# Seven block products in the second feed-forward's up product, reordered token-tile ends, and one product for the index key and the index heads' weights

## The reference, cut to what matters

```python
def conv_ffn(h, w_up, conv_w, conv_b, w_down):
    up = h @ w_up                                   # 512 x 1024 by 1024 x 5632
    up = causal convolution of 3 taps over the tokens(up, conv_w) + conv_b
    val, gate = jnp.split(up, 2, axis=-1)           # 2816 columns each
    return (jax.nn.silu(gate) * val) @ w_down

# in the attention, for its index scores:
qi, ki, wi = index queries (8 heads of 64), index key (64), index heads' weights (8)
score = sum over heads of wi * relu(qi . ki)
```

## Time and profile before

| | |
|---|---|
| time, median of 3 runs | 3673.02 us (3670.11 to 3674.25) |
| the profiled execution | 3677.81 us, of which 3676.0 are the span from the first to the last instruction |
| TensorE busy (PE) | 3330.7 us, 91% of the span |
| VectorE busy (DVE) | 1347.4 us, 37% |
| ScalarE busy (ACT) | 609.4 us, 17% |
| mean granted TensorE clock | 0.966 of full |
| up product matmuls (L2786), both layers | 1408 instructions, 614.2 us |

### The profile page before, as it was taken

One profiled execution on the slowest core, in us unless ns is written; L12 is line 12 of the kernel. 1 busy time (PEld: TensorE's weight loads), 2 busy tenths in 40 slices (PEclk: granted clock), 3 DMA queues, 4 the chain that ended last, 5 costly groups with the idle time before them and its releaser, 6 DMA issues. The chain is left out here.

```text
span 3676.0 us, 48556 instructions
## 1 busy us (share of the span) xinstructions
PE 3330.7 (91%) x21177; PEld 1660.3 (45%) x21177; DVE 1347.4 (37%) x2379; ACT 609.4 (17%) x1204; POOL 8.1 (0%) x40
## 2 busy tenths in 40 slices
PE   6978999898997988888999899999999967999998
PEld 3557787444444333333333344454444434444443
DVE  2245656443022000000000226643666673222256
ACT  2134232110011000000000212242121012211100
POOL 0000000000000000000000000000000000000000
PEclk9989999899997999999999999999999988999999
DMA  6134535211227999999999521103433544212233
GB/s 242 46 122 147 180 124 184 85 57 57 69 98 296 430 430 430 430 431 427 428 428 430 214 73 46 69 7 81 146 116 116 191 142 175 92 51 86 69 131 126
DMA packets 202969, 689.76 MB, mean 188 GB/s; under 512 B 31240, under 2 KB 96252, under 8 KB 176517
## 3 DMA queue, kind: packets, MB, share of 16 engines
q1 hardware_dynamic: 201768, 686.28, 48.0%
q10 hardware_dynamic: 989, 0.36, 0.0%
HBM read 661.94 MB, written 22.31 MB: 186 GB/s over the span
## 5 line engine op out<-in xcount | busy, mean ns | idle before, releaser
L2786 PE MATMUL banks<-h_T,weight_ring 128*128 128x512 f32 x1408 | 614.2, 597 | 5.9 <-PEq L91 5.9
L2786 PEld LDWEIGHTS banks<-h_T,weight_ring 128*128 128x128 f32 x1408 | 268.0, 192 | 338.7 <-issue 338.7
L2061 PE MATMUL banks<-weight_ring,xe_T 128*64 128x512 f32 x1312 | 296.8, 599 | 41.8 <-DMA weight_ring<-in_exp_w 39.5
L2942 DVE SCALAR_TENSOR_TENSOR conv<-banks,cols,conv 128x510 f32<-128x510 f32 (+1 forms) x176 | 131.8, 749 | 334.4 <-ACT conv L2869 329.7
L2061 PEld LDWEIGHTS banks<-weight_ring,xe_T 128*64 128x64 f32 x1312 | 90.5, 137 | 235.4 <-issue 160.3
L2077 PE MATMUL banks<-weight_ring,hid_T 128*64 128x512 f32 x656 | 146.8, 596 | 10.9 <-DMA weight_ring<-in_exp_w 10.9
L2869 ACT ACTIVATE conv<-banks,cols 128x512 f32<-128x512 f32 x88 | 63.7, 773 | 504.4 <-PE banks L2786 504.4
L2382 PE MATMUL banks<-h_T,weight_ring 128*128 128x512 f32 x320 | 142.0, 597 | 0.0
L2061 PE MATMUL banks<-h_T,xe_T 128*64 128x512 f32 x464 | 105.4, 596 | 17.2 <-DMA h_T<-in_exp_w 17.2
L1722 PE MATMUL banks<-h_T,weight_ring 128*128 128x512 f32 x256 | 112.9, 600 | 3.9 <-PEq L91 3.9
L3569 PE MATMUL banks<-weight_ring,h_T 128*128 128x512 f32 x256 | 112.6, 602 | 2.6 <-PEq L91 2.6
(11 more groups left out here) (639 smaller groups left out, 4544.1 us busy)
## 6 DMA issues: line engine op xcount, KB each, us to landing
weight_ring<-in_exp_w SPq DMA_DIRECT2D x123, 2048.0 KB, 15.7
h_T<-in_exp_w SPq DMA_DIRECT2D x41, 2048.0 KB, 15.7
weight_ring<-in_ada_w SPq DMA_DIRECT2D x24, 2048.0 KB, 8.6
weight_ring<-in_ffn_w_up SPq DMA_DIRECT2D x44, 1024.0 KB, 6.7
...
```

The lines of the kernel that those rows point to most:

```text
L2061: mm = pe.matmul(k.ps[64 * half:64 * half + 64, 2 * c + b % 2, :], R.rows[:, e // 2 % 2, kt, (e % 2) * CAP:(e % 2 + 1) * CAP], w[:, r, 512 ...
L2786: mm = pe.matmul(k.ps[:, b + c, :], w[:, c, kt, m * P:m * P + P], hT[:, kt, :], start=kt == 0, stop=kt == 7)
L2942: ins = dve.scalar_tensor_tensor(out=y, in0=k.ps[:, b + c, 0:L - d], scalar=tap(i, c, s), in1=y, op0=ALU.mult, op1=ALU.add)
```

## The change

It has three parts.

**Ends of token tiles.** Shifts move ahead of the root and the norm of the next tile, turns move ahead or into the middle of a product (`middle`), and where the next stage is a feed-forward, its tile 0 is multiplied there, for 256 tokens at a time (`first_unit`). ScalarE loads the square root's table with a dummy instruction first.

```diff
     banks = lambda t: (2 * t, 2 * t + 1)
...
-                        if tail and t >= 2:
-                            T.pe_turn(pe, t - 2, banks(t - 2))
+                        if tail and from_ring and t >= lag:
+                            turn(t - lag)
+                        if tail and not from_ring and t == 2:
+                            turn(0)
...
+            if tail and not from_ring:
+                for t in range(LT):
+                    then(t, (lambda: turn(t + 1)) if t + 1 < LT else None)
+            elif tail and norm:
...
+                    then(t - 2)
+                    turn(t)
...
+            elif tail:
+                then(1, lambda: turn(3))
+                then(3)
...
+            if norm or tail:
+                act.activation(ss[:, 1, 0:1], k.misc[:, 6:7], ACT.Sqrt)
...
                 if tail:
+                    if t >= lag:
+                        T.act_shift(act, t - lag, banks(t - lag))
                     T.act_root(act, t)
-                    if t >= 2:
-                        T.act_shift(act, t - 2, banks(t - 2))
```

```diff
-            pe.matmul(k.ps[:, 2 * t + 1, 0:IDX_HEADS], h, ww[:, kt, 64:72], start=kt == 0, stop=kt == 7)
+            if kt == 3 and middle:
+                middle()
...
+def first_unit(k, n, banks):
+
+    def products(pe, t, middle):
+        two = slice((t - 1) * P, (t + 1) * P)
+        k.ring.wait(pe, n)
+        w = k.ring.chunk(n).rearrange("p (c k n) -> p c k n", c=2, k=8)
+        for c in range(2):
+            for kt in range(8):
+                pe.matmul(k.ps[:, banks[c], two], w[:, c, kt, 0:P], k.hT[:, kt, two], start=kt == 0, stop=kt == 7)
+            if c == 0 and middle:
+                middle()
 
     return products
...
-                    pe.wait_ge(evacuated, s)
+                    k.ring.wait(pe, 1)
+                    w = k.ring.chunk(1)[:, 0:576].rearrange("p (k n) -> p k n", k=8)
                     for kt in range(8):
-                        mm = pe.matmul(out, kiw[:, kt, :], hT[:, kt, :], start=kt == 0, stop=kt == 7)
+                        mm = pe.matmul(out[0:64 + IDX_HEADS, :], w[:, kt, :], hT[:, kt, :], start=kt == 0, stop=kt == 7)
...
+                    if job[0] == "ki":
+                        pe.wait_ge(wi_done, 1)
+                        for t in range(LT):
+                            mm = pe.transpose(k.ps[:, 7, IDX_HEADS * t:IDX_HEADS * t + IDX_HEADS], wi_rows[:, t * P:t * P + P],
+                                              k.sq("eye")[64:64 + IDX_HEADS, 64:64 + IDX_HEADS])
+                        mm.then_inc(wi_turned, 1)
...
+        to_residual(k, lambda kt: oT[:, kt, :], None, [4, 4], 2, False, tail=(k.scales[:, 0, 8:16], k.mod2[:, 0, 24:32], k.hT),
+                    follow=first_unit(k, 2, (0, 1)))
```

```diff
+    bank = lambda i, c: 4 * c if i == 0 and not side else 2 * (i % depth) + c
...
+    plain = FF_T if side else 2
+    half = L // 2
+    low_tokens, high_tokens = slice(0, half), slice(half, L)
+    unit_bank = {1: 5, 6: 6, 7: 7, 5: 1, 2: 0, 4: 4, 3: 2}
+    JOINS = 7
...
-                for i in range(FF_T):
+                for i in range(plain):
...
+                    if i == 0:
+                        pe.sem_inc(products, 1)
+                    else:
...
+                    if side and i == 2:
...
+                    if side and i == 3:
...
+                def block_sum(u, n, left, right):
+                    for kt in range(4):
+                        mm = pe.matmul(k.ps[:, unit_bank[n], low_tokens], left[:, kt, :], right[:, kt, :], start=kt == 0, stop=kt == 3)
+                    mm.then_inc(parts, 1)
...
+                for u in range(len(units)):
+                    a11, a12, a21, a22 = unit_blocks(u)
+                    b11, b12, b21, b22 = token_blocks()
+                    if units[u][1] == 0:
+                        k.ring.wait(pe, units[u][0])
+                    if u:
+                        pe.wait_ge(taken, u)
+                    block_sum(u, 1, a11, b11)
+                    pe.wait_ge(readied, 2 * u + 2)
+                    if u:
+                        pe.wait_ge(joined, JOINS * (u - 1) + 1)
+                    block_sum(u, 6, wsum[:, 1], hsum[:, 1])
+                    if u:
+                        pe.wait_ge(joined, JOINS * (u - 1) + 2)
+                    block_sum(u, 7, wsum[:, 2], hsum[:, 2])
+                    if u:
+                        pe.wait_ge(joined, JOINS * (u - 1) + 4)
+                    block_sum(u, 5, wsum[:, 0], hsum[:, 0])
+                    if u:
+                        pe.wait_ge(joined, JOINS * (u - 1) + 5)
+                    else:
+                        pe.wait_ge(conved, 1)
+                    block_sum(u, 2, a12, b21)
+                    if u:
+                        pe.wait_ge(joined, JOINS * (u - 1) + 6)
+                    block_sum(u, 4, a22, hsum[:, 3])
+                    if u:
+                        pe.wait_ge(joined, JOINS * (u - 1) + 7)
+                    else:
+                        pe.wait_ge(conved, 2)
+                    pe.wait_ge(readied, 2 * u + 3)
+                    block_sum(u, 3, wsum[:, 3], b22)
...
+                def kind(u):
+                    j, c = units[u]
+                    act.wait_ge(joined, JOINS * u + JOINS)
+                    if c:
+                        act.sem_inc(k.ring.used, 1)
+                    act.wait_ge(out_done, 2 * j)
+                    for t in range(2):
+                        ins = act.activation(conv[:, t, c, :], kinds[:, c, t, :], ACT.Identity, scale=tap(2 * j + t, c, 2),
+                                             bias=k.col("ffn_conv_b_2", 44 * layer + 22 * c + 2 * j + t))
+                    ins.then_inc(middle, 1)
...
+                def gates(u):
+                    act.wait_ge(conved, 2 + u + 1)
+                    for t in range(2):
+                        act.activation(silu[:, t, :], conv[:, t, 1, :], ACT.Silu).then_inc(gated, 1)
...
+                        kind(u - 1)
+                    act.wait_ge(parts, 7 * u + 1)
+                    act.activation(m1, k.ps[:, unit_bank[1], low_tokens], ACT.Copy).then_inc(taken, 1)
+                    if u and units[u - 1][1]:
+                        gates(u - 1)
```

VectorE's part, and the side steps:

```diff
+                def token_sums():
+                    b11, b12, b21, b22 = token_blocks()
+                    link(dve.tensor_tensor(hsum[:, 0], b12, b11, ALU.subtract))
+                    link(dve.tensor_tensor(hsum[:, 1], b22, hsum[:, 0], ALU.subtract))
+                    link(dve.tensor_tensor(hsum[:, 2], b22, b12, ALU.subtract))
+                    dve.tensor_tensor(hsum[:, 3], hsum[:, 1], b21, ALU.subtract).then_inc(readied, 1)
...
+                def unit_sums(u):
+                    a11, a12, a21, a22 = unit_blocks(u)
+                    k.ring.wait(dve, units[u][0])
+                    if u:
+                        dve.wait_ge(parts, 7 * (u - 1) + 4)
+                    link(dve.tensor_tensor(wsum[:, 0], a21, a22, ALU.add))
+                    link(dve.tensor_tensor(wsum[:, 1], wsum[:, 0], a11, ALU.subtract))
+                    dve.tensor_tensor(wsum[:, 2], a11, a21, ALU.subtract).then_inc(readied, 1)
...
+                def last_unit_sum(u):
+                    a11, a12, a21, a22 = unit_blocks(u)
+                    if u:
+                        dve.wait_ge(parts, 7 * (u - 1) + 7)
+                    dve.tensor_tensor(wsum[:, 3], a12, wsum[:, 1], ALU.subtract).then_inc(readied, 1)
...
+                def convolve(u):
+                    j, c = units[u]
+                    dve.wait_ge(middle, 2 + u + 1)
+                    for s in (1, 0):
+                        d = 2 - s
+                        for t in range(2):
+                            y = conv[:, t, c, d:L]
+                            link(dve.scalar_tensor_tensor(out=y, in0=kinds[:, c, t, 0:L - d], scalar=tap(2 * j + t, c, s), in1=y, op0=ALU.mult, op1=ALU.add))
+                    dve.sem_inc(conved, 1)
...
+                def unit(u):
+                    j, c = units[u]
+                    ps = lambda n: k.ps[:, unit_bank[n], low_tokens]
+
+                    def put(out, left, right, op=ALU.add):
+                        dve.tensor_tensor(out, left, right, op).then_inc(joined, 1)
+
+                    if u:
+                        last_unit_sum(u)
+                        convolve(u - 1)
+                    dve.wait_ge(taken, u + 1)
+                    dve.wait_ge(parts, 7 * u + 2)
+                    put(u2, m1, ps(6))
+                    dve.wait_ge(parts, 7 * u + 3)
+                    dve.wait_ge(joined, JOINS * u + 1)
+                    put(u3, u2, ps(7))
+                    if c == 0:
+                        multiply(2 * j - 2)
+                        multiply(2 * j - 1)
+                    dve.wait_ge(parts, 7 * u + 4)
+                    dve.wait_ge(joined, JOINS * u + 2)
+                    put(kinds[:, c, 1, high_tokens], u3, ps(5))
+                    put(u2, u2, ps(5))
```

(38 more changed lines are left out.)

146 lines of the change are left out of this document (82 added, 64 removed).

## The result

| | before | after | after, second measurement |
|---|---|---|---|
| median, us | 3672.67 (3670.11 to 3674.25) | 3609.28 (3604.71 to 3612.44) | 3604.78 (3601.11 to 3607.54), before beside it 3672.27 |
| ratio to before | | 0.9823, interval 0.9811 to 0.9836 | 0.9816, interval 0.9803 to 0.983 |
| span of the profiled execution, us | 3676.0 | 3608.2 | 3599.3 |
| TensorE busy, us | 3330.7 | 3281.7 | |
| VectorE busy, us | 1347.4 | 1456.1 | |

The change makes the kernel 1.8% faster: 63 us in the first measurement, 67 in the second; 68.2 were forecast. Both are medians of four executions.

A forecast was written before the change was run, and what follows sets the result against it. TensorE was taken as the bound in the second feed-forward's up products, waiting on VectorE and ScalarE in the tails. Gains 33.2 - 0.5 + 1.5 + 7.0 + 18.1 + 3.9 + 5 = 68.2 us: 3673.0 to 3604.8, range 3597 to 3619.

The forecast's parts named there:

- Seven block products: Second feed-forward's up products: 20 units of 256-column calls at 12.07 us replace tiles of 13.73 us; gain 33.2 us.
- Rival D: Stationary load shows at 256 columns in the units, up to 0.25 us each, 14.0 a unit; 3645 us; 3%.
- VectorE inside a unit: VectorE's work per unit of the second feed-forward, 9.5 to 11.3 us, stays below TensorE's 12.07 us.
- B: VectorE paces the units at about 13.7 us through gaps between waits, so units give nothing; 3638 us; 5%.
- C: VectorE and ScalarE work falls in line with the products, 19.8 us per unit; slower, 3759 us; 3%.
- End of units: After the last unit, a longer chain from last join to second down sums costs 0.5 us, bounds 0 and 1.5.
- Glu tail: Tile 0 of the second feed-forward: TensorE idle 5.8 us, then half clock; gain only 1.5 us.
- Attention tail and side work: Tile 0 of the first feed-forward gains 8.5 us, less 1.5 waiting before turning the state-space inputs; net 7.0.
- Experts' end and first values: First value product starts earlier, TensorE then runs 30.3 us without a stop; gain 18.1 us, 15 if the clock falls.
- key: Index key: TensorE waits for one copy instead of widened weights and four copies, at full clock; gain 3.9 us.
- Mix tail: Before the router products, earlier shift 1 gains 2.5 us at half clock or 8 at full clock; 5 taken.
- Rival A: Tails give nothing: TensorE waits at the next late tile or expert weights start no sooner; 3640 us; 6%.

The follow-up runs named there:

- units_plain: Changed kernel with only the seven-product units undone, tiles 1 to 21 of the second feed-forward as plain 128 x 512 calls: 3643.14 us, 0.9917 of before.
- narrow_calls: Changed kernel with each call of a unit made as two calls of 128 columns, same product: 3618.22 us, 0.9848 of before.
- vector_3_more: Changed kernel with three more VectorE additions of 512 columns behind the last join of each of the 20 units: 3606.5 us, 0.9815 of before.
- vector_6_more: Changed kernel with six more VectorE additions of 512 columns behind the last join of each of the 20 units: 3643.83 us, 0.9914 of before.
- glu_shift_first: Changed kernel, VectorE shifting tile t-2 ahead of its wait for tile t's sigmoid in the tail before the second feed-forward: 3598.71 us, 0.9801 of before.
- before_no_heads: Kernel before the change without the 8-column index-heads products beside the first values: 3663.18 us, 0.9974 of before.
- shift_behind: Changed kernel with shifts again behind root and norm in the three token-tile ends before the first feed-forward: 3614.01 us, 0.9833 of before.
- mix_order: Changed kernel, mix tail only: earlier shifts on VectorE and ScalarE, tile 2's router product ahead of turn 3: 3610.22 us, 0.9823 of before.
- mix_filled: Changed kernel with three unused 512-column calls (six instructions) in TensorE's idle time before the mix tail's second router product: 3606.62 us, single execution.

## Why the prediction was right, and where its terms were off

Forecast 3604.8 us, 3597 to 3619 by its worst and best ends; measured 3609.28 and 3604.78. The large terms came by the mechanism that was written down. That the sum agrees to 2 us is in part luck: the mix tail gave 2.7 less than forecast and the attention's tail with the side work 1.1, while the stretch from the affinities to the first query gave 3.0 more, of which 2.5 stand in routing and experts and in the clock of a few down products, places that the prediction did not count on.

- **Seven block products, 33.2: measured 32.9**, and by units_plain 32.9 in the same place. The price of 256 columns, 0.2156 from the earlier trace rows, held for stationary blocks from sums and weights alike. Rival D (the load shows) is refuted: no idle time, 0.2159; narrow_calls shows that even at half the width the spacing is 0.1117 us, near half. (By D's own 14.0 us a unit its time would be 3643, not 3645.) The estimate from the Trainium skill (TensorE: Matmul & The Clock Gate, Back-to-back issue gap), 86 us lost, did not come: with 128 columns the spacing is 0.112 us, with 256 it is 0.216, with 512 0.429, in proportion to the width.
- **VectorE inside a unit, 9.5 to 11.3: measured 8.9.** Rivals B and C are refuted by the 12.09 us per unit, and by vector_3_more and vector_6_more: at 10.7 of 12.09 us nothing is lost in the units, and at 13.3 only the excess. B and C assumed gaps or a chain in line with the products; there is neither.
- **End of units, -0.5: -0.8**, of which 0.73 is one wait, before the down product at 3470.26.
- **Glu tail, 1.5: 1.5.** Wait 5.55 (5.8 forecast), 16 instructions at half clock 5.8 us (6.05 forecast), tile 1 at full pace behind. glu_shift_first shows that the named cause, the shift queued behind the update of tile 3, is the whole of it. The prediction accepted that place as giving little; one moved line gives 7.1 more.
- **Attention tail and side work, 8.5 - 1.5 = 7.0: measured 5.9.** The wait before the turning of the inputs is 1.08 us. From the output product to tile 1 the tail gives 8.2 us against the first trace, which the forecast started from, and 6.5 against the second: the earlier trace rows had 17.04 us for tile 0, the second trace of the same code 15.36. Behind tile 1 the two traces of before differ by 1.3 us in unchanged code, so what is left of the difference is not told apart. No run undoes this part of the change.
- **Experts' end and first values, 18.1, and key, 3.9: together 22.0; the whole stretch from the affinities gave 25.0.** The part that was forecast came as written: in the first two traces the first value product stands 26.3 us behind the first down product of the stage before (2093.62, 2067.37) and now 16.8 (15.1 in the second trace), 9.5 gained where 9.4 were due, and from there to the first query it is 38.8 instead of 51.7. Of the 13.0 there the 8-column products are 6.9, the key's shorter wait is 2.8, its full clock 1.5 and the full clock of the first value products 2.7 (their 16 instructions took 9.70 us in before_no_heads and take 7.03 now), less 0.9 for one turn more among them. The earlier start is 8.4 us of idle time that is gone (5.91, 1.32 and 1.17) and that turn. The order on ScalarE and VectorE is worth 2.5 of it; the turns' place and the table's load are not told apart.
- **Another 1.5 to 1.8 us lie in routing and experts**, from the affinities to the first down product of the experts' end (952.6 us before, 951.1 and 950.8 after), in code that the change doesn't touch. The two traces of before and the one without the heads' products agree to 0.1 us, but the five further traces with the changed kernel's code up to there have 950.9 to 952.0, so that part of it is scatter: over all seven it is 0.6 to 1.8 us. No run shows its cause.
- **Mix tail, 5: measured 2.3.** This is the term that was mis-sized. The prediction gave 2.5 at half clock and 8 at full clock and took a value between, which neither case gives. The earlier shift came as forecast (shift_behind undoes it and gives 31.9 us back), but the clock did not: mix_order falls to half clock inside a product with no idle time before it, and mix_filled keeps full clock for longer with wide matmuls in the idle time. So the idle time alone is not what costs the clock here; what does is not separated further.
- **Rival A** (tails give nothing): refuted; every tail gave something, the glu tail least. The transfers did start sooner: the experts' first refill went out at 1145.52 instead of 1149.78, 2.8 us earlier when the earlier start of the mix tail (1.4) is taken off.
- **The difference between profile and median, "carried over unchanged":** it did not carry over. The profiled executions of before lay 4.8 and 5.0 above their medians, those of after 0.7 above and near 4 below. A single execution is uncertain by about 5 us in the stretch up to 1080 us alone, more than most terms of the sum. That the forecast met the second median to 0.1 us is luck.

Sum of the measured places: 66.4 against 68.2.
